# Differential attention: combining the exponentials of two heads before the transpose

## What is computed

```python
s = jnp.einsum('bqhcd,bkhcd->bhcqk', qi, k).astype(f32)      # c = 0, 1: the two heads of a pair
s = jnp.where(causal, s, -jnp.inf)
p = jax.nn.softmax(s, axis=-1)
p = p[:, :, 0] - lam * p[:, :, 1]
o = jnp.einsum('bhqk,bkhe->bqhe', p.astype(v.dtype), v)
o = rms_norm(o, sub_g) * (1.0 - lambda_init)
return o.reshape(B, S, H * DIFF_V_DIM) @ w_out
```

## Time and profile before

| | |
|---|---|
| median of 3 runs | 2467.28 us (2465.87 to 2469.51) |
| profiled execution, own time | 2468.71 us |
| its span | 2466.9 us |
| PE busy, weight loads busy | 98%, 83% of the span |
| DVE busy, ACT busy, POOL busy | 70%, 59%, 3% |
| layer 2, steps 1 to 7 (1337 to 1362 us) | PE 25.0 of 25.0, DVE 13.3, ACT 16.5 busy |
| layer 2, steps 8 to 19 (1362 to 1383 us) | PE 19.3 of 21.0, DVE 18.7, ACT 18.1, POOL 10.2 busy |
| the granted TensorE clock | full in both stretches |

### The profile page before, as it was taken

The page is one execution under the profiler, slowest core; times in us unless marked ns, Lnnn a source line. Parts: engine busy times, 40 slices in busy tenths (PEclk is TensorE's granted clock), DMA queues, the critical chain, the costliest instruction groups (busy, mean ns, idle before and its releaser), DMA issues. The chain is left out here.

```text
span 2466.9 us, 32262 instructions
## 1 busy us (share of the span) xinstructions
PE 2421.7 (98%) x12697; PEld 2037.8 (83%) x12697; DVE 1732.9 (70%) x1926; ACT 1446.9 (59%) x1655; POOL 80.9 (3%) x98
## 2 busy tenths in 40 slices
PE   9999999999999999999999999999999999999998
PEld 7889978788888888888778888888888788888887
DVE  5565466888898898888985765666656665557654
ACT  6344454588888888888755554454444544456442
POOL 1000010000000000000000200000000000002000
PEclk9999999999999999999999999999999999999999
DMA  9256552699999999999965265452655165552553
GB/s 318 64 204 205 187 193 71 225 350 352 348 341 348 337 349 351 337 349 340 350 232 205 88 208 193 154 198 91 223 188 196 55 210 188 186 195 91 195 188 102
DMA packets 242222, 555.41 MB, mean 225 GB/s; under 512 B 10824, under 2 KB 36832, under 8 KB 241760
## 3 DMA queue, kind: packets, MB, share of 16 engines
q1 hardware_dynamic: 242016, 552.41, 64.7%
HBM read 551.31 MB, written 1.07 MB: 224 GB/s over the span
## 5 line engine op out<-in xcount | busy, mean ns | idle before, releaser
L1923 DVE TENSOR_TENSOR wlo<-raw,whi 128x2048 fp32r<-128x2048 f32 x486 | 1112.4, 2297 | 454.8 <-ACT whi L1525 454.1
L1525 ACT ACTIVATE whi<-raw 128x2048 fp32r<-128x2048 f32 x488 | 935.2, 1924 | 566.2 <-PE bank L889 139.3
L811 PE MATMUL bank<-whi,xt 128*128 128x512 f32 (+1 forms) x1056 | 311.5, 379 | 3.2 <-DVE xt L1940 1.5
L1148 PE MATMUL bank<-whi,xt 128*128 128x512 f32 (+1 forms) x768 | 222.6, 374 | 3.8 <-DVE wlo L1923 2.9
L811 PEld LDWEIGHTS bank<-whi,xt 128*128 128x128 f32 x1056 | 189.6, 188 | 42.6 <-issue 5.1
L991 PE MATMUL bank<-xt,whi 128*128 128x512 f32 x768 | 209.1, 394 | 0.0
L811 PE MATMUL bank<-wlo,xt 128*128 128x512 f32 (+1 forms) x528 | 197.6, 374 | 0.0
L889 PE MATMUL bank<-whi,h_hi 128*128 128x512 f32 x600 | 186.1, 391 | 0.0
L889 PE MATMUL bank<-whi,h_lo 128*128 128x512 f32 x600 | 185.1, 390 | 0.0
L889 PE MATMUL bank<-wlo,h_hi 128*128 128x512 f32 x600 | 185.1, 390 | 0.0
L1148 PEld LDWEIGHTS bank<-whi,xt 128*128 128x128 f32 x768 | 137.9, 189 | 29.3 <-issue 4.9
(11 more groups left out here) (303 smaller groups left out, 3805.4 us busy)
## 6 DMA issues: line engine op xcount, KB each, us to landing
raw<-in_moe_wg SPq DMA_DIRECT2D x88, 1024.0 KB, 6.2
raw<-in_moe_wu SPq DMA_DIRECT2D x88, 1024.0 KB, 5.9
raw<-in_moe_wd SPq DMA_DIRECT2D x88, 1024.0 KB, 5.9
raw<-in_mlp_w_up SPq DMA_DIRECT2D x64, 1024.0 KB, 5.3
raw<-in_mlp_w_down SPq DMA_DIRECT2D x64, 1024.0 KB, 4.9
raw<-in_diff_w_in SPq DMA_DIRECT2D x24, 1024.0 KB, 5.2
raw<-in_w_in SPq DMA_DIRECT2D x19, 1024.0 KB, 7.5
raw<-in_moba_w_in SPq DMA_DIRECT2D x12, 1024.0 KB, 5.1
```

The lines of the kernel that those rows point to most:

```text
L811: mm = pe.matmul(proj_bank(l, c, t)[:, 0:width], a[:, kx, t * P:(t + 1) * P], b[:, k, :], start=(kx == 0 and i == 0), stop=(kx == KT - 1 a ...
L1148: mm = pe.matmul(bank[b][:, 0:width], a[:, kx, t * P:(t + 1) * P], w[:, k, :], start=(kx == 0 and i == 0), stop=(kx == KT - 1 and i == 2))
L1525: act.activation(whi[u % NH][:, :], raw[u % NR][:, :], ACT.Copy).then_inc(hi_ready[u % NR], 2)
L1923: dve.tensor_tensor(wlo[u % NR][:, :], raw[u % NR][:, :], whi[u % NH][:, :].bitcast(F32), ALU.subtract).then_inc(lo_ready[u % NR], 2)
```

## The change

In the two differential layers, DVE makes one matrix per pair: exponentials of the first head plus those of the second times (minus lambda times the ratio of the sums), in place in `z`. This matrix is transposed, copied and multiplied with the values once per pair, and the result is scaled by the first head's reciprocal.

```diff
+                    if kind == DIFF:
+                        if i % 2 == 0 and 0 <= i - 4 < n:
+                            turn_pair(l, i - 4)
+                        if i % 2 == 1 and 0 <= i - 5 < n:
+                            pair_values(l, i - 5)
...
+            def turn_pair(l, j):
+                s = SOFT0[l] + j
+                pe.wait_ge(combined, SOFT0_DIFF[l] + j // 2 + 1)
...
+                for m in range(3):
+                    mm = pe.transpose(pt_bank(l, j)[:, m * P:(m + 1) * P], z[:, s % 4, m * P:(m + 1) * P], ident)
+                mm.then_inc(pt_done, 2)
...
-                    j = i - 3
-                    if 0 <= j < n and kind == DIFF:
+                    j = i - 4
+                    if 0 <= j < n and kind == DIFF and j % 2 == 0:
                         s = SOFT0[l] + j
-                        act.wait_ge(pt_done, s + 1)
-                        act.activation(pt[:, s % 4], pt_bank(l, j)[:, 0:384], ACT.Copy).then_inc(pt_ready, 1)
+                        act.wait_ge(pt_done, s + 2)
+                        act.activation(pt[:, s % 4], pt_bank(l, j)[:, 0:384], ACT.Copy).then_inc(pt_ready, 2)
...
+            def combine(l, j):
+                s = SOFT0[l] + j
+                dve.wait_ge(p_ready, s + 2)
+                link(dve.reciprocal(rinv[:, :, j:j + 2], sums[:, :, j:j + 2]))
+                d = DIFF_SLOT[l]
+                link(dve.scalar_tensor_tensor(out=rinv[:, :, j + 1:j + 2], in0=rinv[:, :, j + 1:j + 2],
+                                              scalar=lam[:, 10 + d:11 + d], in1=sums[:, :, j:j + 1],
+                                              op0=ALU.mult, op1=ALU.mult))
+                for t, c in enumerate((slice(0, P), slice(P, 3 * P))):
+                    ins = dve.scalar_tensor_tensor(out=z[:, s % 4, c], in0=z[:, (s + 1) % 4, c],
+                                                   scalar=rinv[:, t, j + 1:j + 2], in1=z[:, s % 4, c],
+                                                   op0=ALU.mult, op1=ALU.add)
+                ins.then_inc(combined, 1)
+            def finish_pair(l, j):
...
+                link(dve.tensor_tensor(y[:, :, at], bank[6 + o % 2][:, 0:2 * P].rearrange("p (t c) -> p t c", t=NT), r,
+                                       ALU.mult))
...
+                    if 0 <= j < n and kind == DIFF and j % 2 == 0:
+                        combine(l, j)
...
+                    if 0 <= j < n and kind == DIFF and j % 2 == 1:
+                        finish_pair(l, j - 1)
```

More of the change, by code:

```diff
@@ L64 @@
 SOFT0 = before([NSOFT[k] for k in KIND])
+SOFT0_DIFF = before([NSOFT[k] // 2 * (k == DIFF) for k in KIND])
 STICK0 = before([NSTICK[k] for k in KIND])
@@ L308, in build @@
         proj_done, proj_ev = sem("proj_done"), sem("proj_evacuated")
+        combined = sem("pair_of_heads_combined")
         acc_done = sem("acc_done")
@@ L1406, in soft_heads @@
                     j = i - 4
-                    if 0 <= j < n:
+                    if 0 <= j < n and kind != DIFF:
                         s = SOFT0[l] + j
@@ L1416, in soft_heads, with pair_values @@
                             turn_mixed(l, s)
+            def turn_pair(l, j):
+                s = SOFT0[l] + j
+                pe.wait_ge(combined, SOFT0_DIFF[l] + j // 2 + 1)
+                if s:
+                    pe.wait_ge(pt_ready, s if pt_bank(l, j) is pt_bank(l, j - 2) else s - 2)
+                for m in range(3):
+                    mm = pe.transpose(pt_bank(l, j)[:, m * P:(m + 1) * P], z[:, s % 4, m * P:(m + 1) * P], ident)
+                mm.then_inc(pt_done, 2)
+            def pair_values(l, j):
+                s, o = SOFT0[l] + j, OG0[l] + j // 2
+                if j == 0:
+                    pe.wait_ge(proj_ev, EV0[l] + 10)
+                pe.wait_ge(pt_ready, s + 2)
+                pe.wait_ge(o_read, o - 1)
+                b, w, vcol = bank[6 + o % 2], pt[:, s % 4], head_cols(l, j)[2]
+                v = [h_of(l)[:, t, vcol:vcol + P] for t in range(NT)]
+                pe.matmul(b[:, 0:P], w[:, 0:P], v[0], start=True, stop=True)
+                pe.matmul(b[:, P:2 * P], w[:, P:2 * P], v[0], start=True, stop=False)
+                pe.matmul(b[:, P:2 * P], w[:, 2 * P:3 * P], v[1], start=False, stop=True).then_inc(pv_done, 2)
             def pair_scores(l, j):
@@ L2214, in turn_pairs @@
                 ins.then_inc(rope_done, 1)
+            def combine(l, j):
[12 more added lines that the diff above has]
+            def finish_pair(l, j):
+                h, o = j // 2, OG0[l] + j // 2
+                at = slice(h * P, (h + 1) * P)
+                dve.wait_ge(pv_done, HEAD0[l] + j + 2)
+                r = rinv[:, :, j:j + 1].broadcast_to([P, NT, P])
+                link(dve.tensor_tensor(y[:, :, at], bank[6 + o % 2][:, 0:2 * P].rearrange("p (t c) -> p t c", t=NT), r,
+                                       ALU.mult))
+                for t in range(NT):
+                    ins = dve.tensor_tensor_reduce(o_tmp[:, t, 0], y[:, t, at], y[:, t, at], 1.0, 0.0, ALU.mult, ALU.add,
+                                                   sq[:, t, h:h + 1])
+                link(ins)
+                ask_root(sq[:, :, h], 1.0 / P, NORM_EPS, 2)
+                dve.engine_nop().then_inc(o_read, 1)
             def finish_group(l, order, soft):
```

25 lines of the change are left out of this document (6 added, 19 removed).

## The result

The changed kernel takes 2472.83 us (median of 15 runs, 2470.42 to 2479.4); the kernel before, on the same chip, 2467.31 us (15 runs, 2465.87 to 2471.69). The ratio is 1.0022 with an interval of 1.0015 to 1.0029: slower by 0.22%, 5.5 us. The profiled execution is the fastest of its runs, 2470.42 us with a span of 2468.6, against 2468.71 and 2466.9 before. So the two profiles differ by only 1.7 us, and one has to ask where the rest is.

What follows compares the result with a forecast made beforehand. PE was taken as the bound in steps 1 to 7, DVE from step 8. Losing 2.3 us in layer 2 and 4.7 in both layers, added to the 2467.3 us median, gave 2472.0 us; range 2465.5 to 2475.

Steps and rivals of the forecast that it cites:

- The front part: Layer start up to combining pair 4: fewer transposes and values on PE let pair 4 be combined at 1361.91 us.
- An undisturbed round: From step 8, two heads without POOL's interference: 1.44 + 1.11 + 1.24 = 3.79 us, against 3.43 before.
- The disturbance: From step 8, POOL's second multiplication and DVE's combining instructions exclude each other: a round takes 4.35 us.
- rival (a): No disturbance in the rounds: DVE gets the port when due and POOL yields; 2467.2 us, chance 0.20.
- The sign that was named: In rounds from step 8, the two-column instruction or first over z shows 0.8 to 1 us instead of 0.23 or 0.35.
- The last pair: Layer's end: head 15's exponential waits behind ACT's copies, then L698 blocks; combined 4.36 us after pair 12.
- The start of the output projection: After the heads, its first matmul comes at 1385.54 us instead of 1382.94, 2.60 us later.
- The last turn: End of each layer: later projection start, less the vanished 0.27 us norm wait, loses 2.3 us per layer.
- the sum of 4.7 us: Loss over layers 2 and 5 together, 2.3 us in each, put whole on the median of 2467.3 us.
- (b): PE's saving counts in full, 15.8 us: 2451.5 us; chance 0.10 with everything that ends well below before.
- (c): Held combining instructions cost 0.14 to 0.28 us more each, twelve times: 2473.7 to 2475.4 us, chance 0.20.
- (d): The change does less than it says: pairs are not halved on PE; no size or separate chance given.

Runs made afterwards that it cites:

- e2: Changed kernel with the next two heads' scores ahead of the combined pair's transpose on PE: 2474.54 us, ratio 1.0023 to the kernel before.
- e1: Changed kernel without POOL's second multiplication, the one by the gain: 2468.62 us, ratio 1.0004 to the kernel before.
- e3: Changed kernel with the exponentials of heads 14 and 15 ahead of ACT's copies of pair 12 and turned y: 2466.56 us, ratio 0.9998 to the kernel before.
- e4: Changed kernel with fourteen small matmuls on PE ahead of the turns of pairs 12 and 14: 2472.37 us, ratio 1.0018 to the kernel before.
- B: The edit that puts the next scores ahead of the combined pair's turn on PE; alone on the changed kernel: 2474.54 us, ratio 1.0023 to the kernel before.
- e19: Kernel before with one unused tile of 8 bytes per partition declared behind the gains' tile: 2484.54 us, ratio 1.0069.
- e9: e3 with the gain moved from POOL to ACT's copy of turned y, its tile shrunk: 2480.84 us, ratio 1.0047 to the kernel before.
- e14: Kernel before with the gain moved from POOL to ACT's copy of turned y, its tile shrunk: 2484.23 us, ratio 1.0064.

## Why the prediction held, step by step

**The front part** was right. Pair 4 was to be combined 29.16 us after the layer's first turn of heads (1361.91 less 1332.75); it was at 1360.58 less 1331.55 = 29.03. PE's saving shortens the steps up to 7, and is worth nothing after.

**An undisturbed round** was put at 3.79 us and is 3.82, but two terms are off against each other: a combination takes 1360.58 less 1359.45 = 1.13 us, not 1.24, and from its end to the next row maximum it takes 1362.15 less 1360.58 = 1.57, not 1.44.

**The disturbance** exists where it was put, in the two-column instruction beside L702, and it is what the Trainium skill says in "SBUF — State Buffer", section "Who interferes with whom": by that rule the two exclude each other, whoever is first. The trace agrees: POOL first by 0.18 us, DVE's instruction over 0.02 us after POOL's. The other order was in the trace of the kernel before: POOL's L697, 0.61 us elsewhere, starts 0.18 us behind the weight conversion of the earlier trace rows (L1929, two SBUF inputs, 1358.51 to 1359.74) and takes 1.52.

```profile
1358.68 1.52 POOL L697 TENSOR_TENSOR y<-y,rstd 128x256 f32<-128x256 f32 x1
```

So rival (a) has a point, POOL does yield where DVE is well ahead, but in the rounds POOL comes first (and in e2 a lead of 0.01 us by the recorded start did not make DVE the first). e1, with no second multiplication, shows 0.22 us in all sixteen places. Its size was overrated: 4.35 us for a round, measured 4.15. Two terms were too large. I let the held instruction end 0.09 us after L698, by the case of L2247, where it ends 0.02 after; and the two over `z` take 1364.74 less 1364.07 = 0.67 us, not 0.77. Four rounds are 0.8 us too much. The sign that was named, 0.8 to 1 us for the held instruction, did not come either: it starts 2.90 us after the last combination, not 2.75, since the row maxima come later than put, and so only 0.56 us is left to show.

**The last pair** was put at 4.36 us from one combination to the next, and is 1382.04 less 1377.20 = 4.84 in layer 2 and 2253.68 less 2249.40 = 4.28 in layer 5. Its mechanism, head 15 behind ACT's copies, was right; e3 took it away and won more than any other single edit. The hold by L698 that the sum has in it was not there: the two-column instruction takes 0.22 us in both layers. In layer 5 the reciprocal goes 2252.54 less 2249.40 = 3.14 us after pair 12, not 2.97, and the two-column instruction finds L702 all but done: a wait that is 0.17 us longer stands in for the hold, and the sum is close by luck there. In layer 2 the slow clock made the turns ahead of those copies longer (1.65 against 1.04 us), which no step of the prediction had.

**The start of the output projection** was to be 2.60 us later, counted from the layer's first turn: it is 2.32 (52.51 against 50.19). The wait of the earlier trace rows for the last norm has gone, as said. The last turn was to be 2.3 us later in each layer; it is 1.87 and 3.05. So the sum of 4.7 us met 4.9, but by a smaller round in place of the forecast one and a slow clock that was not in it: without the latter (e4) the layers lose 1.36 and 1.48, 2.8 us. The mechanism was right; that its number came this close is luck.

**What the sum doesn't explain.** The medians differ by 5.5 us, the layers by 4.9 in the profiled executions and by 2.8 without the slow clock. The slow stretches fall differently from execution to execution; the profiled one of the changed kernel happened to miss two that the kernel before has outside the layers, and it is the fastest of its fifteen runs. The mean granted clock of the runs shows the rest of the way: the four runs of the changed kernel at 0.998 took 2470.42 to 2472.39 us, the two lowest, at 0.995 and 0.994, took 2477.2 and 2479.4. On the chip of e1 to e4 the kernel before has a median of 0.999 and e4 of 0.998, where the changed kernel has 0.996. So the changed kernel's runs have more of the slow clock, and the filled waits of e4 take some of it away. The time that this costs in the median was not isolated: e4 is 1 us faster, within the intervals.

**The rivals.** (a), no disturbance, falls by L2254's rows and e1. (b) falls by the rounds. (c), heavier holds, falls: the hold is lighter than assumed. (d) falls too: the change did what it says, as the order of the instructions and PE's counts (362 to 290 in layer 2) show. The chance of 0.43 for slower by over 0.2% and 0.50 for within stand beside a ratio whose interval includes 0.2%, as the text had it. (The two parts that it names for slower, 0.24 and 0.20, make 0.44.)

## What to carry to other kernels

Work taken from an engine that isn't the bound in a stretch buys nothing there, and the waits that it brings are paid in full: look at the order behind the new wait, in the rounds and in the last one apart. Several obstacles in a row hide one another, so an edit that wins nothing alone (B) may win 3.6 us once the others are gone; try the combination before dropping it. And keep all tiles in their places when a tile changes its size, or compare with a kernel in which only the place has moved: here 8 bytes cost three times what the whole change did.

## What the runs showed of the hardware

**Where a stationary operand starts.** Tiles behind one of 8 extra bytes (e19), or behind one 1016 bytes smaller (e9 to e14), cost each matmul that loads its 128 stationary columns from them and streams 512 fp32r columns of an unmoved tile about 5 ns of 390; the results' place in PSUM did not change. The load itself is recorded as 188 ns in both. In the kernel there are 3816 such matmuls (1800 with `h_*`, 960 with `odd_*`, 1056 with `e_*`); their busy times sum to 22.3 us more in e19, and the span is 17.4 us longer. Not everything that moved got slower: the 192 matmuls with `odd_*` and 256 columns took 283 to 284 ns and then 281 to 282, the transposes of 128 columns of `e_hf` stayed at 273 to 274, and the 64 matmuls with `perm_t` as stationary operand and 512 moving columns stayed at 392 to 423. So the place is shown as the cause, and its rule is not. Both shifts leave 8 bytes over a multiple of 64; which boundary counts was not tried. The load and the matmul of one such group, in the kernel before:

```profile
L889 PEld LDWEIGHTS bank<-whi,h_hi 128*128 128x128 f32 x600 | 110.0, 188 | 20.8
L889 PE MATMUL bank<-whi,h_hi 128*128 128x512 f32 x600 | 186.1, 391 | 0.0
```

**Instructions held, and what they have in common.** L2254 (0.56 for 0.22 us) and the pair over `z` in e2 (1.28 for 0.75) read two or more operands from SBUF beside a POOL multiplication that reads SBUF, and L697 (1.52 for 0.61) is POOL's own case. There is also one that reads a single one: `var` in layer 2, 0.55 us where its usual duration is 0.17, beside POOL's L701.

```profile
1385.35 0.55 DVE L1989 TENSOR_SCALAR var<-sq 128x2 f32<-128x2 f32 x1
```

```profile
1385.26 0.61 POOL L701 TENSOR_TENSOR y<-y,rstd 128x256 f32<-128x256 f32 x1
```

POOL's root L678 did not hold anything where it could be seen: in layer 2 it runs from 1384.49 to 1385.19, and the sums of squares L2272, with two SBUF inputs, start at 1384.80 and 1385.02 and take their usual 0.29 us.

```profile
1384.80 0.29 DVE L2272 CUSTOM_DVE_ANT_0 o_tmp<-y 128x128 f32<-128x128 f32 x1
```

**TensorE's clock** fell to 0.50 in the changed kernel's profiled execution after PE had idled 1.45 and then 1.89 us (layer 2), and 1.89, 2.17 and 0.64 us (layer 5). The slow stretch then lies on whatever PE does next: eight turns of `y` in the one and four long matmuls in the other. The idle times alone don't tell when: layer 5's first 1.89 us passed at full clock, and in the kernel before the clock fell at 102 and 1952 us behind idle times of 0.75 and 0.85 us.
